# First norm's scale and offset applied by column to gathered copies and to turned sums; one down matrix loaded in the heads; end norm with a diagonal matrix on TensorE

## The chip, the cores and the metric

The kernel runs on one core of one Trainium2 chip. The metric is the device time of one execution in microseconds (us), the median of several runs. Engines are named as in the profile: PE is TensorE (PEld its weight loads), DVE VectorE, ACT ScalarE, POOL GpSimd, and SPq the queue of SyncE, which issues almost all DMAs.

## The reference, cut to what matters

Two layers (DEPTH 2) over 256 tokens of width 1024, all in float32. In each layer a mixer of three kinds of attention and then a mixture-of-experts part:

```
for l in range(DEPTH):
    mix = hybrid_mixer(x, w_in[l], ..., w_out[l])
    x = layer_norm(ALPHA * x + mix, ln1_g[l], ln1_b[l])      # "first norm"
    ffn = moe_ffn(x, router_w, router_b, moe_w1[l], moe_w3[l], moe_w2[l])
    x = layer_norm(ALPHA * x + ffn, ln2_g[l], ln2_b[l])      # "second norm"
```

`layer_norm` subtracts the row's mean, divides by its standard deviation, then multiplies by g and adds b, both by column. `moe_ffn` sends each token to 2 of 64 experts; an expert computes `(silu(xb @ w1) * (xb @ w3)) @ w2`, with w1 and w3 of 1024 x 256 and w2 of 256 x 1024, 1 MB each. All 64 experts are read in each layer: 192 MB a layer.

## The kernel before

The 256 tokens are two tiles (t = 0, 1) of 128 rows. A layer has a head (projections, attention, output projection, first norm, routing) and then the experts, in 16 batches of NB = 4 experts with 32 slots each. Weights of even batches lie in one set of buffers (`w13_even`, `w2_even`), those of odd batches in another (`w13_odd`, `w2_odd`). `w13(e, k, parity)` and `w2(e, k, parity)` below are the loads of expert k of batch e: two DMAs of 1 MB and one of 1 MB.

The order on SP is written out by hand. In the head it loads w_in, w_out and the weights of batches 0 and 1 as their places come free. The place of w2(1, 3) holds queries and keys of the latent attention until it is done, and after that `ln1_gb`, the scale and offset of the first norm spread over all 128 partitions (`load_ln(sp, l, 0)`, L434 to L436: two DMAs of 512 KB). So w2(1, 3) is loaded only when nobody reads `ln1_gb` any more (L485 to L488), behind the loads of w13 for batch 2. From then on w13 of batch j + 2 waits for each expert's `part_psum` of batch j (expert k of batch j has been used), and w2 of batch j + 2 for `y2_psum` of batch j.

A batch on PE, in order: `up_gate` of the four experts (L1047; for the first expert of the first batch `first_up_gate`, L1064 and L1069), `fold` (L1082), `turn_gated` (L1088), `gather` for the next batch (L1032), `turn_hidden` (L1095), `down` (L1101), and `add_rows` (L1107), which adds the results to the sums `Y`, four PSUM banks that hold the residual of all 256 rows. `gather` picks the rows of x that the next batch's experts want: 16 products, whose stationary operand is `xc[:, t, c, :]`, every eighth column of x. After it, DVE copies one half of the result to `xg` (L1547) and ACT the other (a copy, L1689). Every product of float32 shows as two instructions, a transposition as one.

The first norm is done twice. For the router and for the gathering of the first batch ACT writes the normalised rows without scale and offset, turned by column groups, to `nrm` (L1818), and `gather_first` (L1001) reads those; the scale and offset come by column when DVE and ACT copy the result (`scale_first`, L1583 and L1844). For all that follows, x itself is normalised by rows: tile 0 by DVE (`center_first`, L1462, and `stretch`, L1471), tile 1 by POOL (L585, L590), both with `ln1_gb`. ACT then copies x to Y (`seed`), after PE has set the bits that make later products add to it (`set_bits`, L958). `gather` waits for x of both tiles (`x0_ready`, `x1_ready`).

At the end of the last layer the second norm is applied to Y: ACT, DVE and POOL share the four halves (L1462, L1471, L1720, L599, L601), and SP stores them (L521).

Of the kernel before, what the change touches and what calls it, by code (L numbers as in the profile page):

```python
# [44 lines left out]
POOL_STEPS = 8  # L45
# [35 lines left out]
def program(nc, a, consts, const_at, out):  # L81
# [17 lines left out]
    with ctx:  # L99
# [72 lines left out]
        nrm = moe_mem[:, 2 * DM:3 * DM], moe_mem[:, DM:2 * DM]  # L172
# [13 lines left out]
        ln1_gb = w2_mem[:, 3 * W2:3 * W2 + 2 * DM].rearrange("p (v d) -> p v d", v=2)  # L186
# [10 lines left out]
        y_rows = moe_mem[:, 2 * 2 * FE:2 * 2 * FE + DM]  # L197

# [22 lines left out]

        bits = CT[:, 0:2 * P].bitcast(mybir.dt.bfloat16)
# [30 lines left out]
        class Signal:  # L253
# [17 lines left out]
        ln_in = [Signal(f"ln{turn + 1}_scales_in", 2 * 16) for turn in range(2)]  # L271
# [21 lines left out]
        x0_ready, x1_ready = Signal("x0_ready", 2), Signal("x1_ready", 2)  # L293
# [3 lines left out]
        z_ready, n_ready, y_set, y_seeded = (  # L297
            Signal("z_ready", 5), Signal("n_ready", 2), Signal("y_bits_set", 4), Signal("y_seeded", 4))
# [22 lines left out]
        out_dve, out_pool = Signal("out_dve"), Signal("out_pool")  # L321
# [27 lines left out]
        ln_gb = ln1_gb, ln2_gb  # L349

        def load_ln(eng, l, turn):

            for j, v in enumerate("gb"):
                eng.dma_start(ln_gb[turn][:, j, :], a[f"ln{turn + 1}_{v}"][l].partition_broadcast(P)
                              ).then_inc(ln_in[turn].sem, 16)
# [5 lines left out]
        def _(sp):  # L361
# [3 lines left out]
            for l in range(DEPTH):  # L365
# [32 lines left out]
                if l:  # L398
                    sp.wait_ge(part_psum.sem, b0 * NB + (part_psum.start - 1))
                    load_ln(sp, l - 1, 1)  # L400
# [36 lines left out]
                load_ln(sp, l, 0)  # L437
# [76 lines left out]
                if l == DEPTH - 1:  # L514
                    sp.wait_ge(part_psum.sem, (b0 + m) * NB + (part_psum.start + 2 * NB - 1))
                    load_ln(sp, l, 1)
                sp.reg_add(base, base, m + 2)
            for t, h, sig, n in ((1, 0, out_dve, 1), (1, 1, out_dve, 2), (0, 1, out_pool, 1), (0, 0, out_dve, 3)):
# [7 lines left out]
        def _(pool):  # L526
# [5 lines left out]
            for l in range(DEPTH):  # L532
# [42 lines left out]
                after(pool, l, xT_psum, 9)  # L575
                after(pool, l, n_ready, 2)
                after(pool, l, ln_in[0], 32)
                after(pool, l, routed, 1)
                def by_row(v):
                    return v.rearrange("p (d c) -> p d c", c=DC)  # L580

                turned_back = nrm[1].rearrange("p (c d) -> p d c", c=DC)
                for h in range(2):
                    cols = slice(h * 512, (h + 1) * 512)
                    last = pt(by_row(x[:, 1, cols]), turned_back[:, h * 64:(h + 1) * 64, :],  # L585
                              by_row(ln1_gb[:, 0, cols]), ALU.mult)
                plink(last)
                for h in range(2):
                    cols = slice(h * 512, (h + 1) * 512)
                    pt(x[:, 1, cols], x[:, 1, cols], ln1_gb[:, 1, cols], ALU.add).then_inc(x1_ready.sem, 1)  # L590
# [4 lines left out]

            quarter = slice(512, 1024)
            after(pool, DEPTH - 1, n2_ready, 1)
            after(pool, DEPTH - 1, ln_in[1], 32)
            pt(x[:, 0, quarter], x[:, 0, quarter], ln2_gb[:, 0, quarter], ALU.mult).then_inc(pool_step.sem, 1)  # L599
            pool.wait_ge(pool_step.sem, DEPTH * POOL_STEPS + 1)  # L600
            pt(x[:, 0, quarter], x[:, 0, quarter], ln2_gb[:, 1, quarter], ALU.add).then_inc(out_pool.sem, 1)  # L601
# [3 lines left out]
        def _(pe):  # L605
# [15 lines left out]
            xc = x.rearrange("p t (d c) -> p t c d", c=DC)  # L621
            for l in range(DEPTH):
# [14 lines left out]
                def transpose_z(t, q, to):  # L637

                    zc = x[:, t, q * 256:(q + 1) * 256].rearrange("p (d c) -> p c d", c=2)
# [316 lines left out]
                def set_bits(t, h):  # L956

                    mm(Y[t][h][:, :], bits[:, 0:P], bits, start=True, stop=True, skip_group_check=True  # L958
                       ).then_inc(y_set.sem, 1)

# [31 lines left out]
                set_bits(0, 0)  # L992
                set_bits(0, 1)
                route(1, (6, 7), 8)

                def gather_first(t):
                    nc_ = nrm[t].rearrange("p (c d) -> p c d", c=DC)
                    for c in range(DC):
                        if c == 6:
                            after(pe, l, *((routed, 1) if t else (z_lin, 2)))  # L1000
                        last = mm(first_bank[c // 2][:, c % 2 * P:(c % 2 + 1) * P], nc_[:, c, :], chosen[:, t, :],  # L1001
# [8 lines left out]
                set_bits(1, 0)  # L1010
                after(pe, l, z_lin, 2)
                keep_warm(10, bank[7])
# [7 lines left out]
                set_bits(1, 1)  # L1020
# [4 lines left out]
                def gather(b):  # L1025

                    pe.wait_ge(chosen_ok.sem, b + 1)
                    after(pe, l, x0_ready, 2)
                    after(pe, l, x1_ready, 2)
# [80 lines left out]
                def batch(j, parity, first=False):  # L1110
                    b = b0 + (j + parity)
                    if first:
                        first_up_gate()
                    else:
                        pe.wait_ge(xg_dve.sem, b + 1)
                    for k in range(1 if first else 0, NB):
                        up_gate(j, parity, k)
# [10 lines left out]
                    for k in range(NB):  # L1128
# [71 lines left out]
        def _(v):  # L1200
# [13 lines left out]
            for l in range(DEPTH):  # L1214
# [379 lines left out]
                def batch(j, last_of_all, e_next, first=False):  # L1594
# [8 lines left out]
                    for k in (0, 2):  # L1603
                        if k == 2:

                            after(v, l, x1_ready, 2)
# [315 lines left out]
```

## Time and profile before

| | |
|---|---|
| median of 3 runs | 1169.15 us (1168.12 to 1171.2) |
| the profiled execution | 1169.32 us |
| its span, first to last instruction | 1167.4 us |
| PE busy | 1050.8 us (90%) |
| DVE, ACT, POOL busy | 366.4, 203.8, 32.3 us |
| DMA moved | 442.78 MB, 379 GB/s over the span |
| mean granted PE clock | 0.984 |

Some 1.9 us lie outside the span. A busy share is an average over stages with different limits: in the heads (0 to 150 us and 580 to 727 us of the span) the DMA engines have idle times, and in the batches both PE and DMA are busy nearly all the time, so the share alone doesn't say which of the two sets the end.

### The profile page before, as it was taken

The page shows a single profiled execution, that of the slowest core. Times are in us where ns is not written, and L with a number is a line of the kernel's source. Part 1 is how long each engine was busy: PE and PEld are TensorE (multiplying, and loading weights), DVE is VectorE, ACT ScalarE, POOL GpSimd, SP SyncE. Part 2 cuts the span into 40 slices and gives each one's busy share as a digit, 9 for nine tenths or more (in the row PEclk, how much of TensorE's full clock was granted, in tenths as well). Part 3 has the DMA queues.
Part 4 walks back from the last instruction along what each step waited for, and adds up shares of the span by engine and source line. Part 5 has one row for each costly group of instructions (what it writes and reads, how often), then busy time and mean ns, then how long its engine had stood idle before and what let it go on. Part 6 is the DMA issues. An engine that isn't in the chain of part 4 may idle for free.

```text
span 1167.4 us, 16436 instructions
## 1 busy us (share of the span) xinstructions
PE 1050.8 (90%) x6190; PEld 588.3 (50%) x6190; DVE 366.4 (31%) x1005; ACT 203.8 (17%) x477; POOL 32.3 (3%) x46
## 2 busy tenths in 40 slices
PE   9999989989989898888999999989988998888885
PEld 6665754445544444444456657445544444444442
DVE  4875531111121211111268656311122111111114
ACT  1245221111111111110121532211111111110101
POOL 0010010000000000000000101000000000000001
PEclk9999999999999998999999999999999999998998
DMA  9967699999999999999995776999999999999997
GB/s 306 331 234 288 265 388 421 419 419 422 419 422 421 419 422 420 421 421 417 386 331 202 288 289 265 410 419 420 420 421 421 420 420 420 420 421 420 420 421 264
DMA packets 94088, 442.78 MB, mean 379 GB/s; under 512 B 18272, under 2 KB 37856, under 8 KB 45920
## 3 DMA queue, kind: packets, MB, share of 16 engines
q1 hardware_dynamic: 93760, 441.60, 94.1%
q8 instruction: 26, 0.43, 0.1%
q0 software_dynamic: 144, 0.58, 0.1%
q14 instruction: 14, 0.11, 0.0%
q10 hardware_dynamic: 144, 0.07, 0.0%
HBM read 441.16 MB, written 1.05 MB: 379 GB/s over the span
## 4 chain that ended last, share of the span: by engine, by line
PE 55%; SPq 32%; DVE 5%; DMA 3%; issue 3%; ACT 1%; DVEq 0%; POOL 0%; POOLq 0%
SPq L383 20%; PE bank L1032 10%; SPq L387 10%; PE bank L1047 10%; PE bank L680 9%; PE bank L1101 5%; PE bank L1107 5%; PE bank L806 4%; DMA w_odd<-in_moe_w 3%; SPq L510 2%; PE bank L670 2%; PE bank L1082 1%; PE bank L940 1%; PE bank L776 1%; DVE moe L1635 1%
## 5 line engine op out<-in xcount | busy, mean ns | idle before, releaser
L1032 PE MATMUL bank<-moe,x 128*128 128x128 f32 x960 | 233.1, 402 | 0.0
L1032 PEld LDWEIGHTS bank<-moe,x 128*128 128x128 f32 x960 | 230.7, 334 | 0.0
L1689 ACT ACTIVATE moe<-bank 128x512 f32<-128x512 f32 (+2 forms) x194 | 102.0, 535 | 726.6 <-PE bank L1047 347.0
L1107 PE MATMUL bank<-moe 128*128 128x512 f32 (+1 forms) x264 | 119.5, 593 | 25.2 <-DVE moe L1635 24.1
L1047 PE MATMUL bank<-w_even,moe 128*32 128x512 f32 x992 | 117.1, 616 | 14.2 <-DMA w_even<-in_moe_w 14.2
L1047 PE MATMUL bank<-w_odd,moe 128*32 128x512 f32 x992 | 113.5, 605 | 11.0 <-DMA w_odd<-in_moe_w 11.0
L1608 DVE COPY moe<-bank 128x512 f32<-128x512 f32 x64 | 44.3, 691 | 247.9 <-PE bank L1047 243.0
L1107 PEld LDWEIGHTS bank<-moe 128*128 128x128 f32 x264 | 47.2, 189 | 99.4 <-DVE moe L1635 52.2
L680 PE MATMUL bank<-w_even,w_odd 128*128 128x384 f32 x240 | 81.3, 489 | 0.0
L1047 PEld LDWEIGHTS bank<-w_even,moe 128*32 128x32 f32 x992 | 31.2, 112 | 94.1 <-issue 71.9
L1047 PEld LDWEIGHTS bank<-w_odd,moe 128*32 128x32 f32 x992 | 30.3, 110 | 90.1 <-issue 72.2
L1101 PE MATMUL bank<-w_even,moe 128*32 128x512 f32 x512 | 59.9, 608 | 13.9 <-DVE moe L1627 13.9
L1101 PE MATMUL bank<-w_odd,moe 128*32 128x512 f32 (+1 forms) x544 | 59.8, 571 | 10.5 <-DVE moe L1627 9.6
L680 PEld LDWEIGHTS bank<-w_even,w_odd 128*128 128x128 f32 x240 | 44.5, 190 | 29.1 <-issue 2.0
L1082 PE MATMUL bank<-moe,constants 128*32 128x512 f32 (+1 forms) x272 | 36.3, 603 | 25.4 <-ACT moe L1689 25.4
L1635 DVE COPY moe<-bank 128x512 f32<-128x512 f32 x32 | 22.1, 691 | 111.0 <-PE bank L1101 111.0
L1618 DVE SCALAR_TENSOR_TENSOR moe<-moe,bank 128x256 f32<-128x256 f32 x32 | 13.5, 421 | 136.0 <-ACT moe L1859 136.0
L1547 DVE COPY moe<-bank 128x512 f32<-128x512 f32 x30 | 20.7, 692 | 86.1 <-PE bank L1032 86.1
L1627 DVE COPY moe<-bank 128x256 f32<-128x256 f32 x32 | 13.6, 425 | 101.5 <-PE bank L1095 101.5
L806 PE MATMUL bank<-w_odd 128*128 128x512 f32 x96 | 45.1, 603 | 0.1
L1689 ACT ACTIVATE w_odd<-bank 128x256 f32<-128x256 f32 (+3 forms) x60 | 27.7, 468 | 85.0 <-PE bank L641 27.4
L1101 PEld LDWEIGHTS bank<-w_even,moe 128*32 128x32 f32 x512 | 18.2, 111 | 44.1 <-issue 44.1
(184 smaller groups left out, 822.3 us busy)
## 6 DMA issues: line engine op xcount, KB each, us to landing
w_even<-in_moe_w SPq DMA_DIRECT2D x192, 1024.0 KB, 26.4
w_odd<-in_moe_w SPq DMA_DIRECT2D x188, 1024.0 KB, 26.4
w_even<-in_w_in SPq DMA_DIRECT2D x24, 768.0 KB, 11.5
w_odd<-in_w_out SPq DMA_DIRECT2D x4, 2048.0 KB, 13.8
w_odd<-in_moe_w SPq DMA_DIRECT2D x8, 512.0 KB, 11.2
w_even<-in_w_in SPq DMA_DIRECT2D x4, 416.0 KB, 6.9
w_even<-in_w_in SPq DMA_DIRECT2D x2, 832.0 KB, 8.6
x<-in_x SPq DMA_DIRECT2D x2, 512.0 KB, 5.8
```

Source lines behind the costliest of these rows:

```text
L383: sp.dma_start(w13_slots[parity][k][:, m, :, :].rearrange("p c f -> p (c f)"), (w1, w3)[m][l * NE + e * NB + k]).then_inc(sig.sem, 16)
L387: sp.dma_start(w2_slots[parity][k].rearrange("p c d -> p (c d)"), w2[l * NE + e * NB + k]).then_inc(w2_in[parity][k].sem, 16)
L680: last = mm(to[:, 0:GW], rows[:, c, :], weights[:, c, :], start=fresh and c == 0, stop=c == DC // 2 - 1, skip_group_check=True)
L806: last = mm(mix_bank[t][h][:, :], oT[:, c, t * P:(t + 1) * P], w_out_half[h][:, c, :], start=c == 0, stop=c == DC - 1, skip_group_check=True)
L1032: last = mm(bank[2 + c // 4][:, c % 4 * P:(c % 4 + 1) * P], xc[:, t, c, :], chosen[:, t, :], start=t == 0, stop=t == 1)
L1047: last = mm(bank[k % 2][BLK * q:BLK * (q + 1), :], xg[:, c, BLK * k:BLK * (k + 1)], w[:, :, c, :], start=c < 4, stop=c >= 4)
L1082: last = mm(to[BLK * k:BLK * (k + 1), 0:cols.stop - cols.start], const("fold"), partial[:, k, cols], start=True, stop=True)
L1101: last = mm(to[BLK * k:BLK * (k + 1), 0:hi - lo], hT[:, c, BLK * k:BLK * (k + 1)], w2_slots[parity][k][:, c, lo:hi], start=c == 0, stop=c ...
L1107: return mm(Y[t][h][:, lo - 512 * h:hi - 512 * h], scatter[:, t * P:(t + 1) * P], y_rows[:, lo:hi], start=False, stop=True, skip_group_che ...
L1608: nc.vector.tensor_copy(partial[:, k, :], bank[2 if first and k == 0 else 0][:, :]).then_inc(part_dve.sem, 1)
L1635: nc.vector.tensor_copy(y_rows[:, 0:512], bank[2][:, :]).then_inc(y2_dve.sem, 1)
L1689: return fn(dst, src, ACT.Copy)
```

## The change

- x is written by ACT without scale and offset, turned by column groups (`xc[:, t, c, :]` is then 128 neighbouring columns), from `zb`, the sum of residual and mixer output, which DVE now writes there. `nrm` goes. The gathers of all batches read this x, and the scale and offset are applied at the copies to `xg`, by column: four instructions of 128x128 on DVE in place of one copy of 128x512, and four on ACT.
- Y is seeded from x in another way: `turn_rows(t)` transposes x to Y's banks, ACT (and for four of the chunks of tile 1 DVE) copies it to `seed_mem` with scale and offset by column, and `seed_rows(t)`, 16 products of 64 rows with 64x64 of the identity, writes it back to Y by rows, to every eighth column of a bank. `turn_rows(0)` lies in the head, `seed_rows(0)` and `turn_rows(1)` in the up and gate products of the first batch, `seed_rows(1)` behind its down products.
- In the first batch the gather for the second one moves from ahead of the down products to behind `seed_rows(1)`, and the copies of y wait for `y_seeded`.
- `load_ln(sp, l, 0)`, the row work on DVE and POOL and `set_bits` go. w2(1, 3) is loaded where `ln1_gb` was.
- End norm: for three of the four halves PE adds the offset (identity times offset) and the centred rows times a diagonal matrix of 1/deviation, and ACT copies them out; DVE centres all four and finishes the fourth. POOL does nothing there.

```
 # SP
                 after(sp, l, upT_psum, 2)
-                load_ln(sp, l, 0)
+                load_w2(1, 3, 1)
...
                 load_first(2, 2 * NB, 2, 0, by_matrix=True)
-                after(sp, l, x0_ready, 2)
-                after(sp, l, x1_ready, 2)
-                load_w2(1, 3, 1)
...
 # PE
-            xc = x.rearrange("p t (d c) -> p t c d", c=DC)
+            xc = x.rearrange("p t (c d) -> p t c d", c=DC)
...
+                def turn_rows(t):
+                    for c in range(DC):
+                        last = nc.tensor.transpose(Y[t][c // 4][:, c % 4 * P:(c % 4 + 1) * P], xc[:, t, c, :], ident)
+                    last.then_inc(seed_psum.sem, 1)
+
+                def seed_rows(t):
+                    for c in range(DC):
+                        for h in range(2):
+                            rows = slice(64 * h, 64 * h + 64)
+                            last = mm(Y[t][h].rearrange("p (d c) -> p c d", c=DC)[:, c, :], seed_mem[rows, c, :],
+                                      ident[rows, rows], start=c == 0, stop=True, skip_group_check=True)
+                    return last
...
                 gather_first(0)
-                set_bits(1, 0)
-                after(pe, l, z_lin, 2)
-                keep_warm(10, bank[7])
+                turn_rows(0)
+                keep_warm(7, bank[7])
...
-                set_bits(1, 1)
+                keep_warm(2, bank[7])
...
+                def first_batch():
+                    first_up_gate()
+                    up_gate(0, 0, 1)
+                    after(pe, l, seed_act, 1)
+                    seed_rows(0)
+                    up_gate(0, 0, 2)
+                    up_gate(0, 0, 3)
+                    turn_rows(1)
+                    pe.wait_ge(part_dve.sem, b0 * 2 + 2)
+                    pe.wait_ge(part_act.sem, b0 * 2 + 2)
+                    fold(bank[0], slice(0, 2 * FE)).then_inc(gu_psum.sem, 1)
+                    pe.wait_ge(gated_ok.sem, b0 + 1)
+                    turn_gated(bank[1])
+                    pe.wait_ge(scT_sb.sem, b0 + 1)
+                    turn_hidden(b0)
+                    all_down(0, 0)
+                    after(pe, l, seed_act, 2)
+                    after(pe, l, seed_dve, 1)
+                    seed_rows(1).then_inc(y_seeded.sem, 1)
+                    pe.wait_ge(y2_dve.sem, b0 + 1)
+                    pe.wait_ge(y2_act.sem, b0 + 1)
+                    gather(b0 + 1)
+                    add_all()
...
+            after(pe, DEPTH - 1, ln_in, 32)
+            for t, h, i in by_tensor:
+                mm(bank[i][:, :], ident, ln2_gb[:, 1, h * 512:(h + 1) * 512], start=True, stop=False)
+            for n, (t, h, i) in enumerate(by_tensor):
+                pe.wait_ge(stretch_ok.sem, t + 1)
+                pe.wait_ge(centered.sem, n + 1)
+                mm(bank[i][:, :], stretch_diag[t], x[:, t, h * 512:(h + 1) * 512], start=False, stop=True
+                   ).then_inc(out_psum.sem, 1)
...
 # DVE
                 def copy_gathered(g):
                     v.wait_ge(gathered[0].sem, g + 1)
-                    nc.vector.tensor_copy(xg[:, 0:4, :], bank[2][:, :].rearrange("p (c s) -> p c s", c=4)
-                                          ).then_inc(xg_dve.sem, 1)
+                    for c in range(4):
+                        last = ts(xg[:, c, :], bank[2][:, c * P:(c + 1) * P], g_cols[:, 0, c:c + 1], g_cols[:, 1, c:c + 1],
+                                  ALU.mult, ALU.add)
+                    last.then_inc(xg_dve.sem, 1)
...
-                center_first(1)
                 b0 = batches_before(v, base)
                 place(1).then_inc(chosen_ok.sem, 1)
...
 # ACT
-                    fn(nrm[t].rearrange("p (c d) -> p d c", c=DC), x[:, t, :].rearrange("p (d c) -> p d c", c=DC),
+                    fn(x[:, t, :].rearrange("p (c d) -> p d c", c=DC), zb[t].rearrange("p (d c) -> p d c", c=DC),
                        ACT.Identity, scale=rstd[:, 4 + t:5 + t], bias=shift[:, t:t + 1]).then_inc(n_ready.sem, 1)
...
                 route(1)
+                after(act, l, cols_in, 96)
+                seeds(0, range(DC))
```

## Rows read from the trace of the kernel before

**Rows 1.** The page: DMA by slice, rates by slice, and the chain by engine.
```profile
DMA  9967699999999999999995776999999999999997
GB/s 306 331 234 288 265 388 421 419 419 422 419 422 421 419 422 420 421 421 417 386 331 202 288 289 265 410 419 420 420 421 421 420 420 420 420 421 420 420 421 264
...
PE 55%; SPq 32%; DVE 5%; DMA 3%; issue 3%; ACT 1%; DVEq 0%; POOL 0%; POOLq 0%
```

**Rows 2.** Windows of layer 0: stretch, engines busy, PEclk, DMA share, GB/s.
```profile
60.00:65.00 5.00, 5.00 (x18) 2.73 (x18) 3.83 (x7) 0.29 (x1) 0.00 (x0) 1.00 0.05 19
...
150.00:155.00 5.00, 5.00 (x62) 2.11 (x62) 3.30 (x6) 1.61 (x4) 3.25 (x3) 1.00 0.64 234
155.00:160.00 5.00, 4.21 (x34) 1.91 (x22) 2.77 (x9) 2.60 (x6) 0.00 (x0) 1.00 1.02 426
```

**Rows 3.** Timeline of SP's queue: start, us, issues.
```profile
54.64 0.33 SPq L354 DMA_DIRECT2D w_odd<-in_ln_g  x1
...
150.76 6.89 SPq L383 DMA_DIRECT2D w_even<-in_moe_w  x8
157.77 0.37 SPq L387 DMA_DIRECT2D w_odd<-in_moe_w  x1
...
177.80 5.94 SPq L383 DMA_DIRECT2D w_odd<-in_moe_w  x8
...
727.18 6.97 SPq L383 DMA_DIRECT2D w_even<-in_moe_w  x8
...
754.22 5.94 SPq L383 DMA_DIRECT2D w_odd<-in_moe_w  x8
```

**Rows 4.** Chain that ended last, PE's pieces in layer 0: start, us, what.
```profile
64.93 0.65 PE bank L749 x8
65.57 0.43 PE bank L753 x8
...
124.03 0.95 PE bank L641 x8
...
127.56 1.73 PE bank L951 x16
...
146.69 2.05 PE bank L1001 x16
...
158.96 7.61 PE bank L1032 x32
...
167.66 3.67 PE bank L1101 x32
...
172.11 3.70 PE bank L1107 x8
```

**Rows 5.** Timeline of PE, DVE and ACT around the first batch of layer 0.
```profile
145.20 0.75 DVE L1462 SCALAR_TENSOR_TENSOR x<-x,small,w_odd 128x512 f32<-128x512 f32 x1
145.22 0.43 PE L1014 MATMUL bank<-moe,constants 128*128 128x64 f32 x2 [0.17 <-DVE moe L1505]
...
147.84 1.37 DVE L1583 TENSOR_SCALAR moe<-bank,small 128x128 f32<-128x128 f32 x4
148.54 1.50 ACT L1844 ACTIVATE moe<-bank,small 128x128 f32<-128x128 f32 x4 [4.87 <-PE bank L1001]
...
157.52 1.07 PE L1082 MATMUL bank<-moe,constants 128*32 128x512 f32 x8 [0.79 <-ACT moe L1689]
...
159.06 0.42 DVE L1618 SCALAR_TENSOR_TENSOR moe<-moe,bank 128x256 f32<-128x256 f32 x1 [1.95 <-ACT moe L1859]
...
166.61 0.60 ACT L1689 ACTIVATE moe<-bank 128x512 f32<-128x512 f32 x1 [7.23 <-PE bank L1032]
```

**Rows 6.** Timeline at the end of the last layer.
```profile
1156.20 1.13 PE L1107 MATMUL bank<-moe 128*128 128x256 f32 x4 [0.50 <-ACT moe L1689]
...
1161.24 2.93 DVE L1471 SCALAR_TENSOR_TENSOR x<-x,small,w_even 128x512 f32<-128x512 f32 x3
```

**Rows 7.** A window late in the batches of layer 0, columns as in rows 2.
```profile
536.00:538.00 2.00, 1.92 (x12) 0.59 (x16) 0.00 (x0) 0.00 (x0) 0.00 (x0) 0.50 0.99 410
```

More of the change, by code:

```diff
@@ L1186, in _ @@
                 m, b0 = start_batches(pe, base, l)
-                batch(0, 0, first=True)
+                first_batch()
                 batch(0, 1)
@@ L1627, in batch @@
                     nc.vector.tensor_copy(hT, turned_h).then_inc(hT_sb.sem, 1)
+                    if first:
+                        after(v, l, seed_psum, 2)
+                        for c in range(4, DC):
+                            last = ts(seed_mem[:, c, :], Y[1][1][:, (c - 4) * P:(c - 3) * P], g_cols[:, 0, c:c + 1],
+                                      g_cols[:, 1, c:c + 1], ALU.mult, ALU.add)
+                        last.then_inc(seed_dve.sem, 1)
                     if not last_of_all:
@@ L1673, in _ @@
                 else:
[L1675 to L1677 removed]
+                    after(v, l, ln_in, 32)
+                    for t in range(NT):
+                        for h in range(2):
+                            cols = slice(h * 512, (h + 1) * 512)
+                            stt(out=x[:, t, cols], in0=Y[t][h][:, :], scalar=mean_var[:, t, 0:1], in1=ln2_gb[:, 0, cols],
+                                op0=ALU.subtract, op1=ALU.mult).then_inc(centered.sem, 1)
+                    v.wait_ge(centered.sem, 4)
+                    after(v, l, pow_out, 5)
+                    stt(out=x[:, 1, 512:], in0=x[:, 1, 512:], scalar=rstd[:, 7:8], in1=ln2_gb[:, 1, 512:],
+                        op0=ALU.mult, op1=ALU.add).then_inc(out_dve.sem, 1)
         @block.scalar
@@ L1839, in copy_gathered @@
                     act.wait_ge(gathered[1].sem, g + 1)
-                    copy(xg[:, 4:8, :], bank[3][:, :].rearrange("p (c s) -> p c s", c=4)).then_inc(xg_act.sem, 1)
-                after(act, l, cols_in, 96)
+                    for c in range(4, DC):
+                        last = fn(xg[:, c, :], bank[3][:, (c - 4) * P:(c - 3) * P], ACT.Identity,
+                                  scale=g_cols[:, 0, c:c + 1], bias=g_cols[:, 1, c:c + 1])
+                    last.then_inc(xg_act.sem, 1)
                 def scale_first(c):
@@ L1901, in _ @@
                 act.reg_add(base, base, m + 2)
-                normalise(l, 0, (0, 1) if l < DEPTH - 1 else (1,))
+                if l < DEPTH - 1:
+                    normalise(l, 0)
+            for t in range(NT):
+                after(act, DEPTH - 1, pow_out, 4 + t)
+                fn(stretch_diag[t], ident, ACT.Identity, scale=rstd[:, 6 + t:7 + t]).then_inc(stretch_ok.sem, 1)
+            for n, (t, h, i) in enumerate(by_tensor):
+                act.wait_ge(out_psum.sem, n + 1)
+                copy(x[:, t, h * 512:(h + 1) * 512], bank[i][:, :]).then_inc(out_act.sem, 1)
 def kernel(**inputs):
```

163 lines of the change are left out of this document (59 added, 104 removed).

## The prediction, made before the changed kernel had run

> **What bounds the kernel now.** I read the chain of waits first, then the DMA lines by slice, then windows around the first batches. The chain gives PE 55% and SP's queue 32% [rows 1]. Taken literally it says that PE sets the time in the first batches of each layer and the loads only after them. The DMA lines say otherwise: from the seventh slice on they stand at 9 and at 419 to 421 GB/s [rows 1], and the windows show where that begins: share 0.64 from 150 to 155 us, 1.02 from 155 on [rows 2]. A transfer that PE releases into a queue which is still full doesn't start sooner when PE is sooner. So from the first load of batch 2 to the end of the layer the time is bytes at 420 GB/s, 2.5 us for each MB of weights (1.049 MB), as long as the queue never runs dry. The heads are different: there the DMA engines idle (share 0.05 from 60 to 65 us) [rows 2], and PE and the routing chain set the pace. What counts is therefore three things: the head, the bytes in the full stretch, and whether the queue stays full between the loads that PE releases.
>
> **Bytes.** w2(1, 3), issued at 157.77 in the full stretch, moves to where the first norm's scale was issued, 54.64 [rows 3]. There it takes the place of as many bytes (two loads of 512 KB), with an idle stretch right behind. The full stretch loses one load: -2.5 us a layer.
>
> **Routing.** DVE's row work for tile 0 goes. Its second half (0.75 us from 145.20) stood between the selection and the placing of tile 1, which also waits for the rank product, ended at 145.65 [rows 5]. The placing, which began behind the row work at about 146.05, can begin at about 145.75; with PE's two extra warming products behind it, -0.3 us a layer. Its first half, and POOL's part, lay beside other work: 0. `turn_rows(0)` costs eight transpositions, 0.95 us by the row of eight [rows 4], and replaces a `set_bits` and three warming products at about 0.1 us an instruction: 0. ACT's eight copies for tile 0 take 3.0 us (four take 1.50 [rows 5]); its wait of 4.87 us ahead of 148.54 [rows 5] shows it free from 143.7: 0.
>
> **Gather.** The stationary operand of L1032 has a stride of eight elements: 32 instructions take 7.61 us, 238 ns each. The same product from neighbouring columns, L1001, takes 2.05 us for 16, 128 ns each [rows 4]. With x in the new order each gather takes about 4.0 us. The copies by column cost more: DVE 1.37 us for four, hidden in the second half of the gather; ACT 1.50 where one took 0.60 [rows 5], and the down products wait for it, so some 0.7 us more are exposed. PE gains about 2.8 us a batch. In the full stretch that is worth nothing by itself (27 us lie between the first loads that two batches release [rows 3], and the twelve loads of a batch take 30); it matters in the first two batches. The Trainium skill, "SBUF — State Buffer", in its note on cachelines, says that accesses which each reach a new 16-byte line pay a penalty; stride eight of float32 does, and the two rows agree.
>
> **The queue between w13(2) and w13(3).** This is what the step hangs on. The queue fills at 150.76; from the windows (234 GB/s for 5 us, then full) it is as if it ran at 420 GB/s from 152.3. Before, it held 13 loads until 184.8 and w13(3) came at 177.80 [rows 3], 7 us early. Now it holds 12, until 182.2. w13(3) waits for the second batch's first expert, and PE gets there by another way:
> - `seed_rows(0)`: +S. `turn_rows(1)`: 0.95, of which 0.8 covers the wait of `fold` for ACT [rows 5]: +0.2.
> - From the end of `fold` to the down products it took 9.1 us (158.6 to 167.66) with the gather of 7.61 in it [rows 4]. Without the gather the chain through ACT and DVE is bare: 0.4 for the tanh, two DVE steps of 0.42 [rows 5], the turning 0.3, its copy 0.4, handoffs 0.6, together 2.5 us: -6.6.
> - `seed_rows(1)`: +S. Then the copies of y as before, and the gather, 4.0, now ahead of the adding. The copies to `xg` finish beside `add_rows`, 3.70 us [rows 4]: 0.
>
> Together 2S - 2.4 later, so w13(3) is issued at 175.4 + 2S. The first bytes follow about 1.5 us behind an issue (150.76 to 152.3). The queue is empty for 2S - 5.3 us, if that is above zero. Layer 1 has the same 27.04 us between the two issues (727.18, 754.22) [rows 3], so I take the same there. The head's 0.3 shifts all alike.
>
> **S.** One `seed_rows` is 32 instructions: 64 rows by 128 columns stationary, 64 columns moving, upper and lower half in turn. No row shows it. Nearest: L749, also 64 rows in alternating halves, 8 in 0.65 us, 81 ns each: S = 2.6. Below: L753, four groups of 32 rows, 54 ns: 1.7. Above: L951, all 128 rows with 64 moving columns, 108 ns: 3.5 [rows 4]. What none of them has is an output to every eighth column of PSUM. If that is slowed as the strided weight load is, 238 ns: 7.6. I take 2.6, since the halves match; the empty time is then just zero, and I put 0.3 us a layer for standing on the edge.
>
> The Trainium skill, "SBUF — State Buffer", same note, says that any non-contiguous PSUM access pattern significantly slows matmuls. This speaks against `seed_rows`; it gives no factor, and the upper end, S = 7.6, was worked out without it. No trace here shows such a write.
>
> **End.** Before, the last DVE step ended at 1164.17 (1161.24 + 2.93) [rows 6]. Now PE has six products of 128x512, 0.93 us each (3.70 for four [rows 4]), from 1157.4 at the earliest (its last adding ends at 1157.33 [rows 6]): 1162.9, handoffs and ACT's copy of 0.6 make about 1163.8 to 1164.0. I take -0.2; from -0.6 (PE at its best) to +0.8 (scales landing late). The rest behind it, the stores, is as before.
>
> **Sum.** Profiled execution 1169.32, span 1167.4 (1.9 around it), the median is 1169.15. Per layer -2.5 - 0.3 + 0.3 = -2.5; twice -5.0; end -0.2: 1164.1 against the own time, and against the median (0.15 lower) 1164.0. I say 1164.1.
>
> **Rivals.**
> 1. *Seeding at the pace of full weight loads.* S = 3.5: 1.7 us empty in each layer in place of 0.3: 1166.9. For it: these instructions have 128 stationary columns like L951, and its 108 ns don't depend on the moving 64. Against: L749 has these too and takes 81.
> 2. *The strided output makes it slower than before.* Place: both `seed_rows`. At S = 7.6, 10 us empty a layer: 2 x (10 - 2.8) - 0.2 = +14, 1183. It decides from the point where 2S - 5.3 exceeds 2.9, S = 4.1 (128 ns an instruction); slower by over 0.3% from S = 5.0. For it: the stride of eight on the load side costs nearly a factor of two. Against: only the 64 moving columns are written, half of what L1032 has, so even a doubled write may hide behind the next weight load.
> 3. *PE's clock.* PE now waits longer for loads in late batches, 5 to 6 us of 30. After an idle stretch of 2 us it ran at 0.50 [rows 7], which is 1.2 GHz. In the middle the slack covers it; if it falls in a layer's last batch, 1 to 2 us a layer on top: 1167.1.
> 4. *The chain read literally*: PE has 55% of the span, 642 us; less some 300 for the heads that is 13 batches of 26 us, and a faster gather gives 2.8 us in each: 1133. Against: the slices of the batches hold no idle DMA time that could be won [rows 1], and the bytes stay. I leave it 1 in 100.
>
> **Chances.** Forecast (S from 1.7 to 2.9): 0.54. Rival 1: 0.18. Rival 2: 0.17, of which 0.04 near the deciding point. Rival 3: 0.09. Rival 4 and unknown: 0.02. 0.3% is 3.5 us and about what a measurement here can tell from no change. Faster by more: the forecast and a part of rivals 1 and 3, 0.58. Within: most of rivals 1 and 3, a little of rival 2, 0.25. Slower: 0.17. Range: low end S = 1.7 and the end at its best, 1163.0, less the spread of runs, 1162.6; the high end takes in rivals 1 and 3 and the mild part of rival 2, 1169.5. The likeliest case's own range is 1162.6 to 1165.6.
>
> **What would show it.** A gather's 32 instructions in about 4 us; those of a `seed_rows` in 2.6; loads of w13(3) issued about 30 us behind those of w13(2), where it was 27.04; a window around that moment at full DMA share. Wrong if S is above 3.5, if a window there shows idle DMA, if w2(1, 3) delays another load in the head, or if the last batch of a layer shows PEclk at 0.5.

## The result, and the profile after

The changed kernel takes 1161.47 us, the median of 4 runs (1160.14 to 1163.38), beside 1168.76 us for the kernel before in the same comparison: ratio 0.9937, with a 95% interval of 0.9926 to 0.9949. It is faster by some 7 us. The profiled execution took 1162.24 us, its span is 1160.4 us. The forecast was 1164.1 us with a range from 1162.6 to 1169.5: the sign is right, the time lies 1.1 us below the range.

The page of the changed kernel, rates by slice and the chain by engine:

```profile
GB/s 305 337 234 290 271 394 418 420 420 421 421 420 420 421 421 420 421 420 419 384 334 195 281 299 264 405 419 420 420 420 420 420 420 421 420 420 421 420 420 274
...
SPq 52%; PE 37%; issue 4%; DVE 4%; DMA 3%; ACT 1%; POOL 0%; DVEq 0%; POOLq 0%
```

In the slices that lie wholly in the batches the rates are 418 to 421 GB/s, as before within 3 GB/s, while PE's share of the chain fell from 55% to 37% [rows 1]. So PE's share before was no measure of what a faster PE would win. The same stretch of time as in [rows 2], and one in the middle of the batches, in the windows of the changed kernel:

```profile
150.00:155.00 5.00, 5.00 (x62) 2.65 (x58) 2.27 (x9) 0.60 (x1) 0.00 (x0) 1.00 0.96 362
...
300.00:330.00 30.00, 22.39 (x159) 9.79 (x159) 5.83 (x17) 4.03 (x9) 0.00 (x0) 0.94 1.01 421
```

The same middle stretch of the kernel before, with PE 4.3 us busier and the same rate:

```profile
300.00:330.00 30.00, 26.72 (x165) 13.99 (x158) 6.11 (x15) 3.72 (x7) 0.00 (x0) 1.00 1.01 420
```

SP's queue after, the lines that answer to [rows 3]:

```profile
53.64 0.33 SPq L386 DMA_DIRECT2D w_odd<-in_moe_w  x1
...
149.10 8.99 SPq L382 DMA_DIRECT2D w_even<-in_moe_w  x8
165.71 2.52 SPq L386 DMA_DIRECT2D w_even<-in_moe_w  x4
177.73 5.96 SPq L382 DMA_DIRECT2D w_odd<-in_moe_w  x8
...
722.87 8.98 SPq L382 DMA_DIRECT2D w_even<-in_moe_w  x8
...
751.51 5.94 SPq L382 DMA_DIRECT2D w_odd<-in_moe_w  x8
```

The load of w2(1, 3) stands at 53.64 and no longer at 157.77. Between the issues of w13(2) and w13(3) lie 28.63 us in layer 0 and 28.64 in layer 1, where it was 27.04. The first batch in the chain that ended last, PE's pieces, the answer to [rows 4]:

```profile
144.00 0.43 PE bank L990 x2
...
145.38 1.79 PE bank L978 x16
...
151.64 1.93 PE bank L938 x32
...
157.14 1.02 PE bank L931 x8
...
161.96 3.64 PE bank L1075 x32
165.60 1.96 PE bank L938 x32
...
168.47 3.83 PE bank L1006 x32
172.31 3.44 PE bank L1081 x8
```

L938 is `seed_rows`, 60 ns an instruction; L931 is `turn_rows(1)`; L1006 the gather, 3.83 us where it was 7.61; L1075 the down products, L1081 `add_rows`. The placing of tile 1, in the timeline, to be read beside [rows 5]:

```profile
144.47 0.22 DVE L1512 SCALAR_TENSOR_TENSOR moe<-bank,moe 128x64 f32<-128x64 f32 x1 [0.53 <-PE bank L990]
```

The rank product (L990) ends at 144.43; the placing follows 0.04 us behind. Last the end, the answer to [rows 6]: PE's last down products in the timeline of the kernel before, then in that of the changed kernel, and the last pieces of its chain.

```profile
1155.06 0.64 PE L1101 MATMUL bank<-w_odd,moe 128*32 128x256 f32 x8
```

```profile
1149.09 0.64 PE L1075 MATMUL bank<-w_odd,moe 128*32 128x256 f32 x8
```

```profile
1151.41 2.84 PE bank L1201 x6
1154.26 2.59 PE bank L1205 x6
...
1156.87 0.60 ACT x L1687
```

**The sum by stages.** Taken from the profiles: head 0 runs from the end of the first 24 warming products to the first load of w13(2), stretch 0 from there to the first load of w_in for layer 1, head 1 and stretch 1 likewise (to PE's last down products), the tail from there to the end. In us, the kernel before against three profiles of the changed kernel (this one and those of e1 and e12 below):

| | before | after | e1 | e12 |
|---|---|---|---|---|
| warming | 5.46 | 4.40 | 4.59 | 5.36 |
| head 0 | 143.93 | 143.33 | 143.31 | 143.28 |
| w13(2) to w13(3), layer 0 | 27.04 | 28.63 | 30.18 | 30.32 |
| stretch 0 | 418.67 | 416.33 | 417.20 | 417.23 |
| head 1 | 157.75 | 157.44 | 156.87 | 157.42 |
| stretch 1 | 427.88 | 426.22 | 424.46 | 425.16 |
| tail | 12.34 | 11.31 | 11.40 | 11.08 |

The mean of the three, against before and e3 (whose heads and batches are those of before; its tail is not, so the tail is taken against before alone): heads -0.75 and -0.5, stretches -1.9 and -2.2, tail -1.1, together -6.4 us.

One boundary of this table moves by itself. The first load of w_in is issued 8.2 us ahead of PE's last down products of layer 0 in the kernel before and in e1, but 8.8 and 8.7 us ahead in the profiled execution and in e12. With the start of those last down products as the boundary, which stretch 1 has already, the same profiles, and those of e2 and e4 (below) read more evenly:

| | before | e3 | after | e1 | e12 | e2 | e4 |
|---|---|---|---|---|---|---|---|
| w13(2) to the last down products, layer 0 | 426.89 | 427.20 | 425.11 | 425.38 | 425.96 | 427.19 | 427.20 |
| from there to w13(2), layer 1 | 149.53 | 149.49 | 148.66 | 148.69 | 148.69 | 148.68 | 149.00 |

Read so, the heads gained 0.75 and 0.83 and the stretches 1.6 and 2.2; the sum is the same.

### The profile page after: what moved, and what is told of

It reads as the page before. It is cut to its first block, busy times and chain, and to the rows that moved or that the text cites. A ratio compares the mean times of both kernels' runs of the same rounds, so it can differ in the third digit from the quotient of the medians.

```text
span 1160.4 us, 16892 instructions
## 1 busy us (share of the span) xinstructions
PE 966.9 (83%) x6350; PEld 482.2 (42%) x6350; DVE 379.9 (33%) x1093; ACT 237.2 (20%) x587; POOL 18.7 (2%) x36
## 4 chain that ended last, share of the span: by engine, by line
SPq 52%; PE 37%; issue 4%; DVE 4%; DMA 3%; ACT 1%; POOL 0%; DVEq 0%; POOLq 0%
SPq L382 33%; SPq L386 16%; PE bank L653 9%; PE bank L1021 5%; PE bank L779 4%; PE bank L1075 2%; SPq L506 2%; DMA w_odd<-in_moe_w 2%; PE bank L1006 2%; PE bank L1081 2%; PE bank L643 2%; PE bank L913 1%; PE bank L749 1%; PE bank L764 1%; PE bank L1056 1%
## 5 line engine op out<-in xcount | busy, mean ns | idle before, releaser
L1687 ACT ACTIVATE moe<-bank 128x512 f32<-128x512 f32 (+2 forms) x164 | 84.2, 523 | 592.3 <-PE bank L1021 416.6
L1021 PE MATMUL bank<-w_odd,moe 128*32 128x512 f32 x992 | 124.9, 644 | 43.9 <-DMA w_odd<-in_moe_w 43.9
L1021 PE MATMUL bank<-w_even,moe 128*32 128x512 f32 x992 | 122.3, 631 | 36.7 <-DMA w_even<-in_moe_w 36.7
L1593 DVE COPY moe<-bank 128x512 f32<-128x512 f32 x64 | 44.3, 692 | 295.1 <-PE bank L1021 290.6
L1081 PE MATMUL bank<-moe 128*128 128x512 f32 (+1 forms) x264 | 119.3, 593 | 24.0 <-DVE moe L1626 22.9
L1006 PE MATMUL bank<-moe,x 128*128 128x128 f32 x960 | 117.1, 282 | 1.9 <-DVE moe L1626 1.9
L1006 PEld LDWEIGHTS bank<-moe,x 128*128 128x128 f32 x960 | 114.9, 199 | 2.2 <-issue 2.2
L1081 PEld LDWEIGHTS bank<-moe 128*128 128x128 f32 x264 | 47.2, 189 | 96.4 <-DVE moe L1626 49.2
L1075 PE MATMUL bank<-w_even,moe 128*32 128x512 f32 x512 | 58.2, 594 | 27.4 <-ACT moe L1843 17.7
L1075 PE MATMUL bank<-w_odd,moe 128*32 128x512 f32 (+1 forms) x544 | 59.6, 570 | 24.3 <-issue 15.2
L1626 DVE COPY moe<-bank 128x512 f32<-128x512 f32 x32 | 22.1, 692 | 138.5 <-PE bank L1075 130.0
L1843 ACT ACTIVATE moe<-bank,small 128x128 f32<-128x128 f32 x120 | 45.2, 457 | 102.1 <-PE bank L1006 102.1
L1056 PE MATMUL bank<-moe,constants 128*32 128x512 f32 (+1 forms) x272 | 38.9, 643 | 23.7 <-ACT moe L1687 23.7
L1536 DVE TENSOR_SCALAR moe<-bank,small 128x128 f32<-128x128 f32 x120 | 41.0, 404 | 33.9 <-PE bank L1006 33.9
L779 PE MATMUL bank<-w_odd 128*128 128x512 f32 x96 | 44.7, 601 | 0.0
L1075 PEld LDWEIGHTS bank<-w_even,moe 128*32 128x32 f32 x512 | 18.0, 109 | 56.1 <-issue 56.1
```

Source lines behind the costliest of these rows:

```text
L779: last = mm(mix_bank[t][h][:, :], oT[:, c, t * P:(t + 1) * P], w_out_half[h][:, c, :], start=c == 0, stop=c == DC - 1, skip_group_check=True)
L1006: last = mm(bank[2 + c // 4][:, c % 4 * P:(c % 4 + 1) * P], xc[:, t, c, :], chosen[:, t, :], start=t == 0, stop=t == 1)
L1021: last = mm(bank[k % 2][BLK * q:BLK * (q + 1), :], xg[:, c, BLK * k:BLK * (k + 1)], w[:, :, c, :], start=c < 4, stop=c >= 4)
L1056: last = mm(to[BLK * k:BLK * (k + 1), 0:cols.stop - cols.start], const("fold"), partial[:, k, cols], start=True, stop=True)
L1075: last = mm(to[BLK * k:BLK * (k + 1), 0:hi - lo], hT[:, c, BLK * k:BLK * (k + 1)], w2_slots[parity][k][:, c, lo:hi], start=c == 0, stop=c ...
L1081: return mm(Y[t][h][:, lo - 512 * h:hi - 512 * h], scatter[:, t * P:(t + 1) * P], y_rows[:, lo:hi], start=False, stop=True, skip_group_che ...
```

## The experiments

Each time stands beside that of the kernel before on the same chip, which over these comparisons was 1168.5 to 1169.0 us. Experiments are edits of the changed kernel unless the text says otherwise.

**e1_again, e12_after_third: the changed kernel again.**

> The changed kernel once more, to size the result and to see what its profile does in the first 6 us. Compared with before, the changed kernel's profile gained 7.1 us: 1.06 in the 24 warming instructions at the very start (4.40 us where they took 5.46), 0.9 in the heads, 4.0 in the two full stretches, 1.0 behind the last load. Theory A: the 1.06 us at the start are chance (when PE's clock comes up), so that over many runs the gain is about 6 us, ratio 0.9949, and the warming takes either time in either kernel. Theory B: it belongs to the changed program, and the ratio stays at 0.9937.

> The changed kernel a third time, for the stages of one more profile: head 143.3 of layer 0 (behind the warming) against 143.9 and 144.2 before, stretch of layer 0 416.3 to 417.2 against 418.7 and 419.0, head of layer 1 156.9 to 157.4 against 157.7, stretch of layer 1 424.5 to 426.2 against 427.1 to 427.9, end 11.3 to 11.4 against 12.3. Theory: each lies in or near these; the warming instructions take anything from 4.4 to 5.5 us. Rival (the spans are chance): a stage falls back to where it was before.

Measured: 1160.99 us, ratio 0.9943 (0.9929 to 0.9956), and 1162.45 us, ratio 0.9943 (0.9928 to 0.9958). The gain stands. What the profiles of e1 and e12 add is PE's clock. The first batch in windows of e1:

```profile
161.00:163.00 2.00, 1.19 (x9) 0.40 (x12) 1.65 (x6) 0.52 (x2) 0.00 (x0) 0.72 1.00 422
163.00:165.00 2.00, 2.00 (x16) 0.64 (x12) 0.53 (x4) 0.00 (x0) 0.00 (x0) 0.50 1.02 430
```

and the down products there, in its chain:

```profile
162.12 5.20 PE bank L1075 x32
```

Granted clock 0.50 is 1.2 GHz, the lower of its two levels; the down products took 5.20 us instead of 3.64, and w13(3) came 30.18 us behind w13(2). Before it fell, PE had been busy only in pieces for some 3 us: this is the chain through ACT and DVE that the gather used to cover. That chain isn't needed for a fall, though: in e4 below, where the gather still stands there, the clock fell too, at 167 us, in a pause of 0.9 us that followed 7.61 us of gather, and the down products took 5.35 us. The DMA share in both windows is 1.00 or more. Some 18 us later the delay reaches the queue: e12's half-microsecond windows from 181.5 to 182.5 us show 262 and 229 GB/s, in e1 no such dip shows.

The clock fell in a second place. In the last batch of layer 0 PE waited 3.15 us for weights in the profiled execution of the changed kernel and ran at 0.50 behind that, and in e12 likewise; in e1 it waited 0.76 us and kept its clock. The same two microseconds, first of the changed kernel, then of e1:

```profile
558.00:560.00 2.00, 2.00 (x12) 0.23 (x4) 0.00 (x0) 0.00 (x0) 0.00 (x0) 0.50 0.98 402
```

```profile
558.00:560.00 2.00, 1.91 (x17) 0.48 (x17) 0.00 (x0) 0.00 (x1) 0.00 (x0) 1.00 1.01 418
```

**e2_w2_late: the load back in its old place.**

```
-                after(sp, l, upT_psum, 2)
-                load_w2(1, 3, 1)
...
                 load_first(2, 2 * NB, 2, 0, by_matrix=True)
+                load_w2(1, 3, 1)
```

> The changed kernel with w2(1, 3) issued where it was before, behind w13 of batch 2. Theory of the prediction (bytes at 420 GB/s in a stretch whose queue never runs dry): +2.5 us a layer, +5.0 in all, about 1166.5. Rival (PE's faster gather is what gave the time, the load hides either way): no difference, 1161.5.

Measured: 1166.81 us, ratio 0.9987 (0.9978 to 0.9996). That gives back 5.3 us of the gain of 7 (5.8 against e1, which ran in the same comparison). SP's queue shows the load again behind w13(2), ahead of w2(2):

```profile
150.30 8.98 SPq L382 DMA_DIRECT2D w_even<-in_moe_w  x8
159.32 0.46 SPq L386 DMA_DIRECT2D w_odd<-in_moe_w  x1
168.60 1.75 SPq L386 DMA_DIRECT2D w_even<-in_moe_w  x4
```

Its stretches are 418.98 and 427.33 us, 2.1 and 2.0 longer than the mean of the changed kernel's (1.7 and 2.0 with the later boundary). All the faster gathers, the new copies, the seeding and the end norm are still in this kernel; against the kernel before they leave it 1.7 us (0.5 to 2.6 by the interval).

**e3_end_only: the kernel before, with the new end norm alone** (diagonal matrices and centring as in the changed kernel, POOL's part gone; its heads and batches are those of before).

> The kernel before with nothing changed but the end norm (diagonal matrix on PE, ACT copies out, POOL idle). By the two profiles the end gained 1.0 us: ratio 0.999. By my prediction 0.2 us: 0.9998. Both lie near what timing can tell, so the reading is in the profile: from the last wait for a load of w2 to the last instruction 12.35 us before, 11.3 after.

Measured: 1167.56 us, ratio 0.9992 (0.9983 to 1.0001). The interval alone doesn't tell it from no change; its tail does, 11.34 us where it was 12.34 (12.32 in e4, which has the old end; 11.08 to 11.40 in every profile with the new one). The end of its chain:

```profile
1156.35 2.84 PE bank L1197 x6
1159.19 2.59 PE bank L1201 x6
...
1161.80 0.60 ACT x L1700
```

Six products in 5.43 us, to the hundredth what the changed kernel shows.

**e4_center_later: the kernel before, the row work of tile 0 behind the placing.**

```
-                center_first(1)
                 b0 = batches_before(v, base)
...
                 scale_first(5).then_inc(xg_dve.sem, 1)
+                center_first(1)
```

> The kernel before with nothing changed but the second half of DVE's row work of tile 0 (center_first(1)) moved from ahead of the placing of tile 1 to behind the first scaled copies. Theory: from the end of the warming to the first load of batch 2 it takes 0.4 us less than before, 143.5 to 143.7 in place of 143.9 to 144.2, and the same 0.4 less in layer 1 (157.3 in place of 157.7), which is most of what the heads of the changed kernel gained. By the prediction's 0.3 a layer: 143.8 and 157.4. Rival: nothing, because another wait takes its place.

One execution: 1168.15 us. The placing in its timeline, behind a rank product that begins at 145.19 and takes 0.43:

```profile
145.66 0.23 DVE L1524 SCALAR_TENSOR_TENSOR moe<-bank,moe 128x64 f32<-128x64 f32 x1 [0.53 <-PE bank L1014]
```

The heads are 143.51 and 157.23 us, 0.55 and 0.5 less than the mean of before and e3. In layer 0 that is most of the 0.75 that the head gained. In layer 1, with the later boundary, it is 0.5 of 0.83. The other 0.3 us lies ahead of the routing: eight products of the output projection (L806, in the changed kernel L779) take 4.04, 4.00 and 3.98 us there before, in e3 and in e4, and 3.70 us in the changed kernel, e1, e12 and e2. What makes that difference isn't known.

**e5_hold_12, e6_hold_30: PE held back between `seed_rows(1)` and the gather**, by 12 and by 30 warming products.

```
                     seed_rows(1).then_inc(y_seeded.sem, 1)
+                    keep_warm(12, bank[0])      # e6: 30
```

> The changed kernel with 12 warming products (24 instructions, 2.8 us) on PE behind seed_rows(1), so that the first loads of batch 3 are released 2.8 us later. Theory of the prediction: the queue had 2S - 5.3 = 1.4 us to spare at the measured S of 1.95, so it runs dry for 1.4 us a layer: +2.8 us, about 1164.3. Rival 1 (PE's path sets the time): +5.7. Rival 2 (the queue has far more to spare): 0.

> The changed kernel with 30 warming products (7.1 us) behind seed_rows(1). Theory: 7.1 less 1.4 to spare, 5.7 us of empty queue a layer, +11.4 us, about 1173, slower than the kernel before by 0.3%. Where S would have been 5.5 us, this is what the change would have cost. Rival (something other than the queue sets the time): less than half of it.

Measured: e5 1164.3 us, ratio 0.9964 (0.995 to 0.9978); e6 1172.61 us, ratio 1.0027 (1.0019 to 1.0036). In e5 the twelve products partly lie in a wait for the copies of y: w13(3) comes 30.31 us behind w13(2), only 1.7 more than in the changed kernel, and its profiled span, 1160.0 us, shows no loss, though the median over the runs is 1.9 to 3.3 us above the changed kernel's. Its runs spread from 1161.86 to 1165.42; what the slower ones had isn't known, so that the median falls on the forecast is no proof of it. In e6 the distance is 35.99 us, and the windows show what follows:

```profile
180.00:182.00 2.00, 2.00 (x11) 1.28 (x10) 0.84 (x4) 1.24 (x4) 0.00 (x0) 1.00 0.86 348
182.00:184.00 2.00, 2.00 (x6) 0.61 (x4) 0.00 (x0) 0.27 (x1) 0.00 (x0) 1.00 0.08 33
184.00:186.00 2.00, 2.00 (x21) 0.68 (x24) 0.00 (x0) 0.00 (x0) 0.00 (x0) 1.00 0.00 0
186.00:188.00 2.00, 2.00 (x27) 0.54 (x19) 0.69 (x1) 0.20 (x1) 0.00 (x0) 1.00 0.46 66
```

PE is busy all the while and the DMA engines stand still for 5 us and more. By the formula of the prediction the queue is dry for what the distance has above 29.9 us (182.2 less 1.5 less 150.76), 6.1 here; the whole kernel lost 11 us against the changed one, 5.6 a layer. The same stretch of the changed kernel:

```profile
180.00:182.00 2.00, 2.00 (x24) 0.64 (x20) 0.69 (x1) 0.00 (x0) 0.00 (x0) 1.00 1.02 410
182.00:184.00 2.00, 1.19 (x13) 0.19 (x8) 0.00 (x0) 0.60 (x1) 0.00 (x0) 1.00 1.03 426
```

**e7_slow_batches: 15 warming products in every later batch**, ahead of the waits for the gathered rows.

```
                     turn_hidden(b)
+                    keep_warm(15, bank[0])
                     pe.wait_ge(xg_dve.sem, b + 2)
```

> The changed kernel with 15 warming products (30 instructions, 3.5 us) ahead of the down products of every batch but the first and the last: PE's batch is then as long as before the change. Theory: 0, at most +1 from the end of a layer, since the loads set the time. Rival (the chain read literally, PE sets the time in some 13 batches): +46 us.

Measured: 1162.76 us, ratio 0.9944 (0.9931 to 0.9956): no loss that can be told. The window in the middle shows PE as busy as before the change:

```profile
300.00:330.00 30.00, 27.04 (x190) 13.46 (x186) 6.78 (x18) 4.62 (x10) 0.00 (x0) 1.00 1.01 420
```

PE can be given back all that the gathers saved, and the time stays. The chain read literally (rival 4) is refuted. The clock in the middle of the batches costs nothing either: it is 1.00 in this window here and 0.94 in the changed kernel, and both take the same time.

**e8_stride: the routing writes x in its natural order, and the gathers read every eighth column again.** Scale and offset are still applied at the copies.

```
-                    fn(x[:, t, :].rearrange("p (c d) -> p d c", c=DC), zb[t].rearrange("p (d c) -> p d c", c=DC),
+                    fn(x[:, t, :], zb[t],
...
-            xc = x.rearrange("p t (c d) -> p t c d", c=DC)
+            xc = x.rearrange("p t (d c) -> p t c d", c=DC)
```

> The changed kernel with x in the old column order (gathers and turn_rows read every eighth column, as the gathers did before). Gather back to 7.6 us. Theory: 3.8 us for the gather and up to 0.9 for turn_rows(1) come on top ahead of the first loads of batch 3, less 1.4 to spare: 3.3 us of empty queue a layer; gather_first(1) in the head takes 1.9 more. Together +5.2 a layer, +10.4, about 1172. If the order of x were only worth PE time that the loads hide: +3.7, from the heads alone.

Measured: 1191.11 us, ratio 1.0204 (1.018 to 1.0228). Slower as expected, but by 29.6 us against the changed kernel and not by 10.4. Its chain:

```profile
147.63 3.80 PE bank L978 x16
...
165.92 5.34 PE bank L1075 x32
...
174.14 7.89 PE bank L1006 x32
```

The expectation counted the gather of the second batch and left out the rest. Both gathers of the first batch (L978) are in the head, 3.80 us each where the changed kernel has 1.79. The down products of the first batch ran at 5.34 us. w13(3) comes 34.45 us behind w13(2), and the windows show two dry stretches in place of one, the second ahead of w2(3), which is issued at 209.53 (194.07 in the changed kernel). One window of the first, one of the second, and the last microseconds of PE in layer 1:

```profile
185.00:190.00 5.00, 5.00 (x46) 1.46 (x48) 0.69 (x1) 0.60 (x1) 0.00 (x0) 1.00 0.29 79
...
210.00:215.00 5.00, 4.79 (x20) 1.85 (x24) 0.65 (x3) 0.06 (x1) 0.00 (x0) 1.00 0.89 331
...
1172.00:1178.00 6.00, 5.54 (x48) 2.19 (x44) 2.49 (x4) 0.38 (x1) 0.00 (x0) 1.00 0.03 12
```

The last line is the third loss. PE needs 26.7 to 29.9 us a batch here, with the long gathers, the new copies and down products of 4.96 to 6.62 us where the clock fell (3.67 elsewhere); the loads of a batch take 30. It gains too little on them to make up for the late start, and works 6 us on when the DMA engines have finished. By the stages: head 0 +3.1, stretch 0 +6.1, head 1 +6.6, stretch 1 +12.8, against the mean of the changed kernel. The chain by engine says it too:

```profile
PE 89%; DVE 4%; ACT 3%; issue 3%; POOL 0%; DVEq 0%; POOLq 0%
```

How much of the 29.6 us belongs to the clock and how much to the gathers wasn't told apart. What follows: the new order of x doesn't win time by itself in the full stretch, but with the seeding now ahead of the second gather the kernel can't do without it.

**e10_plain_write: `seed_rows` writes neighbouring columns.** The residual then lies in the wrong columns of Y; the work is the same.

```
-mm(Y[t][h].rearrange("p (d c) -> p c d", c=DC)[:, c, :], seed_mem...
+mm(Y[t][h][:, c * 64:(c + 1) * 64], seed_mem...
```

> The changed kernel, but seed_rows writes each product to 64 neighbouring columns of PSUM and not to every eighth; the residual then lies in the wrong columns. Theory (a write with stride costs this form nothing, the weight loads set its pace): 32 instructions in 1.9 to 2.0 us as with the stride. Rival (the stride slows it and the plain form is faster than any row of before): 1.7 us or less.

One execution: 1163.31 us. Its chain:

```profile
152.87 1.93 PE bank L938 x32
...
168.53 1.96 PE bank L938 x32
```

1.93 and 1.96 us, the same as with every eighth column. The strided output costs nothing here, so rival 2 had no ground.

**e9_warm_gap, e11_two_gaps: filling the bare chain of the first batch**, to keep the clock up. e9 puts four warming products behind `turn_gated`; e11 has these and three more behind `seed_rows(1)`.

```
                     turn_gated(bank[1])
+                    keep_warm(4, bank[3])
...
                     seed_rows(1).then_inc(y_seeded.sem, 1)
+                    keep_warm(3, bank[0])       # e11 only
```

> The changed kernel with 4 warming products (8 instructions, 0.95 us) on PE between turn_gated and the wait for the scatter copy in the first batch, where PE otherwise stands idle for 1.1 us of a stretch of 3. In five of ten first batches of the profiles so far the granted clock fell to 0.50 there and the down products took 5.2 us where they take 3.64, so that w13(3) came 30.2 us behind w13(2) and not 28.6. Theory: with the gap filled it comes 28.6 behind in both layers, and the queue never runs dry; worth 0.3 us in a layer where the clock would have fallen (1.7 less 1.4 to spare), so 1161.0, ratio as before within noise. Rival: the clock falls for another reason, and 30.2 is seen again.

> With one gap filled the granted clock fell one gap later in layer 0 (behind seed_rows(1), the gather took 5.46 us in place of 3.8) and w13(3) still came 30.4 behind w13(2). Here the second gap, the wait for the copies of y, is filled too, with 3 products (0.7 us of a wait of 0.9). Theory: the clock stays, w13(3) comes 28.6 to 28.8 behind in both layers; the time is that of the changed kernel or up to 0.6 us less, which timing can't tell. Rival: it falls again elsewhere, since PE is still idle for about 1 us in the stretch.

Measured: e9 1162.37 us, ratio 0.9941 (0.9928 to 0.9955); e11 1162.92 us, ratio 0.9953 (0.994 to 0.9967). In e9 the down products held 3.64 us in both layers, but in layer 0 the clock fell one gap later, and the gather paid:

```profile
166.79 1.96 PE bank L938 x32
...
169.66 5.46 PE bank L1006 x32
```

w13(3) still came 30.42 us behind w13(2), so the theory that this one gap decides fell. With both gaps filled the profile shows 28.63 and 28.64 us, and the time is no better, so the fallen clock of the first batch costs little. How little shows between w13(2) of layer 0 and w13(2) of layer 1, in one profile each: 573.74 us in e5, where the clock fell in neither the first nor the last batch of layer 0; 573.77 and 573.83 in the changed kernel and e11 (last batch alone); 574.07 and 573.62 in e1 and e7 (first alone); 574.33, 574.65 and 574.79 in e9, e12 and e10, where it fell in both. A fall in one of the two costs at most 0.3 us, falls in both 0.6 to 1.0 us; why they don't simply add wasn't tested. No version measured better than the changed kernel.

## Why the prediction came out as it did

What sets the time was read rightly. What failed is the size of terms in the sum: it gave the end, the two heads and the base 0.9, 1.0 and 0.6 us too many, and the two full stretches 0.6 us too few.

**Right: what sets the time.** Bytes at 420 GB/s from the first load of batch 2 on, the heads, and whether the queue stays full in between. e2 shows the first (5.3 us come back with one load a layer), e7 that PE's time in the later batches isn't in the sum, e6 that the queue runs dry when w13(3) is later by some 7 us. The working of w13(3)'s moment held: with the measured S = 1.95 it gives 27.04 + 3.9 - 2.4 = 28.5 us behind w13(2), measured 28.63. The gather took 3.83 us for about 4.0 predicted.

The Trainium skill, "SBUF — State Buffer", note on cachelines, says that accesses which each reach a new 16-byte line pay a penalty. e8 against the changed kernel agrees on the load side, 7.6 to 7.9 us a gather against 3.6 to 3.8. The same note says that any non-contiguous PSUM access pattern significantly slows matmuls. That didn't show: 60 ns an instruction with and without the stride (e10). For this output of 64 float32 columns at stride eight the measurement decides.

**Wrong: S.** Taken 2.6, bounded below by 1.7, measured 1.93 to 1.96: in the range, and nearer to L753 (54 ns) than to L749 (81 ns) [rows 4]. L749 was taken for its two halves; it also moves 128 columns, these products 64. With S = 1.95 the queue has 1.4 us to spare, so the +0.3 a layer for standing on the edge had no ground in the pace. It stands, however, against something that was measured: one load a layer was taken as -2.5, and the stretches shrank by 1.6 and 2.2 (e2 gives 1.7 and 2.0 for the load alone). That the two misses nearly cancel is luck: -2.2 net a layer predicted, -1.9 measured. The fallen clock is a part of it in layer 0: the distance is then 30.2 to 30.3 against 29.9, and against the profiled execution, whose first batch kept its clock, stretch 0 took 0.27 us longer in e1 and 0.85 in e12 (later boundary). Without it the load is still worth 0.3 to 0.6 less than its bytes, and why isn't settled.

**Wrong: the end, -0.2 predicted, -1.1 measured.** This is the largest miss in a single term, and e3 shows it alone (-1.0). From PE's last down products to the end of ACT's last copy it took 8.38 us (1149.09 to 1157.47), where 8.75 to 8.95 were predicted and DVE had needed 9.11 before (1155.06 to 1164.17, [rows 6]): the six products took 5.43 us for 5.55, and between them and the copy lie 0.02 us where 0.25 to 0.45 was allowed for handoffs. This part alone, 0.73 (9.11 less 8.38), is more than the best case of 0.6. The other 0.3 is behind it: from that copy to the end 2.9 us, before 3.2, which the prediction had left "as before". What made that shorter isn't known.

**Wrong: the heads, -0.3 a layer predicted, -0.75 and -0.83 measured.** The mechanism that was named is right, and e4 shows it alone; its size was 0.4 to 0.5. The placing now follows its product by 0.04 us, where the prediction allowed 0.1, and before it began at 146.09. The chain runs through the two extra warming products, but from the start of the rank product to the end of the gather it takes 3.17 us with them and 3.13 in e4 without. The rest, 0.3 us in layer 1, is the shorter output projection, which the sum left out.

**Wrong: the base.** The sum was made from the profiled execution, 1169.32 us, and the median of the three runs agreed with it. Over later comparisons the kernel before is at 1168.5 to 1169.0. Its profile has a slow start, 24 warming products in 5.46 us; in the 14 profiles of this case the same 24 take 4.36 to 5.46, whatever the kernel. Base 0.6 too high, end 0.9, heads 1.0, less 0.6 in the stretches: 1164.1 becomes 1162.2. The measured medians are 1161.0, 1161.5 and 1162.5. The rest, some 0.6 us, is within the scatter of stretch 1 (424.5 to 426.2 us in profiles of the same kernel) and is not assigned. The low end of the range held one term's best case and the spread of runs, and no room for three terms that were each too cautious in the same direction.

**The rivals.** Rival 1 (seeding at 108 ns) fell with 60 ns. Rival 2 fell with e10. Rival 4 fell with e7. Rival 3, the clock, had the event right and the price too high. In layer 0 the last batch showed PEclk at 0.50 in 2 of 3 profiles of the changed kernel, which the prediction had named as a sign of being wrong, and it fell in the first batch too, in 2 of 3 in layer 0 and in none in layer 1 (with the same work, in e7 and e10 also in layer 1). The rival said 1 to 2 us a layer; a fall in one of the two batches cost at most 0.3 us, in both 0.6 to 1.0, and the spare 1.4 us of the queue take up most of the first batch's. In the middle it costs nothing as long as PE has slack; in e8 it hadn't.

**Open.** Why the clock falls in some executions of the same program and not in others; the parts of e8's loss; the 0.3 to 0.6 us of a load's worth; the 0.3 us of the output projection and the 0.3 us behind the last copy.

## What to carry to other kernels

Where slices show the DMA engines full, ask what the queue holds when PE releases the next load, and count how late that load may come: here 1.4 us were left, and the 7.4 us by which e6 delayed it cost more than the whole gain. A share in the chain of waits is no price: the same DMA rate stood beside 55% and 37% of PE. And when a sum has several small terms that are each rounded to the careful side, put their common error into the range.

## What the runs showed of the hardware

- Products of 64 rows in alternating halves, 128 stationary and 64 moving columns of float32, take 60 ns an instruction, written to neighbouring or to every eighth column of PSUM.
- The stationary operand at stride eight: 238 to 247 ns an instruction; from neighbouring columns 112 to 128 ns.
- PE's granted clock can fall to 0.50 in a gap of 3 us in which it is busy in pieces, and it fell as well in a pause of 0.9 us that followed 7.61 us of gather (e4); four products in that gap moved the fall to the next one (e9) in layer 0, and seven in two gaps left 28.63 us in the one profile (e11).
